# Norm hand-overs, a halved first load, routing by counting, and single waits in a two-block fp32r transformer kernel on one core

## The chip, the cores and the metric
One core of a Trainium2 chip (trn2) runs the whole program in one launch. The metric is the device time in microseconds. Three timed runs of the kernel before gave 1406.56, 1406.8 and 1409.7 us; the median is 1406.8. A separate profiled execution took 1410.64 us, with a span of 1408.7 us from its first to its last instruction.

## The reference, cut to what matters
256 tokens of width 1024 pass through two blocks of two layers each, all in f32.

```python
x = x + even_mix(rms_norm(x, even_norm) @ even_w_in) @ even_w_out        # two attentions, 16 heads each
x = x + odd_mix(rms_norm(x, odd_norm) @ odd_w_in) @ odd_w_out            # retention, 4 heads
x = rms_norm(x, final_norm)
h = layer_norm(x, ln_in_g, ln_in_b)
for l in range(2):
    h = layer_norm(ALPHA * h + hybrid_mixer(h, ...), ln1_g[l], ln1_b[l])
    f = swiglu(h, ffn_wg, ffn_wu, ffn_wd) if l == 0 else moe_swiglu(h, router, wg, wu, wd)
    h = layer_norm(ALPHA * h + f, ln2_g[l], ln2_b[l])

# moe_swiglu: top 2 of 8 experts per token
logits = h @ w_router
top_v, top_i = lax.top_k(logits, 2)
w_top = softmax(top_v)
out = sum over e of gate[:, e] * swiglu(h, wg[e], wu[e], wd[e])
```

## The kernel before
All weights lie in the order of their use as 275 slots of 128 x 2048 f32 (1 MB). A slot is loaded by SP into a raw buffer (two buffers before the experts, four in them). ScalarE (ACT) rounds it to fp32r (`w_hi`), VectorE (DVE) subtracts to get the rest (`w_lo`), and TensorE (PE) multiplies three pairs of parts: hi x hi, lo x hi, hi x lo (`parts_mm`, L592 to L594). Activations are split the same way into `x_hi`, `x_lo` and `y_hi`, `y_lo`. Four decoded slots exist at a time, three in the expert stage. SP may load a raw buffer again once `w_lo` of its last slot is made. Each engine's program is written out by hand in its own order; `ahead(s)` on ACT and on DVE prepares the slot four (three) places later and waits until PE has used the slot that stood there. So the place of an `ahead` call decides which other work of that engine stands behind a late weight.

PE also issues filler matmuls whose results nobody reads: `keep_busy` (L611) around the norms, with counts in `BUSY`, and nine at the start (L891).

Seven norms lie between the stages. Norm 1 (after the even layer) and norm 2 (after the odd layer) are done by `residual_norm`, norms 3 to 5 by `scaled_norm`; both end in `rest_of_norm`. There are two tiles of 128 tokens (t) and two halves of 512 columns (b). For each, DVE adds the matmul result (`joined`), sums (`summed`), and per tile asks POOL for a root (`ready`), centres (`centre`), scales (`finish`, which counts `n_h`); PE turns the rows (`turn_rows_of`), ACT makes `x_hi` (`hi_x`, `n_hi`), DVE makes `x_lo` (`low_part`, `n_lo`), and the next stage's matmuls begin in `begin`. For norm 2 DVE also squares and multiplies by `final_gain` before the statistics.

Other places that the change touches. Start: `const`, `xT`, slot 0, slot 1 and `x` are loaded in this order. After slots 0 to 3, PE needs `small_lo` for 32 narrow matmuls (`small_rows`), then slot 4, then `fold_rows(0)`, which waits for ACT's copy `rows24` (L1385). Even layer output: PE waits for `y_split` of 8 ahead of output slots 4 and 5. Odd layer: ACT copies the value banks at every second V slot (L1418); PE waits for `r_lo` of 4 ahead of the output slots. Sparse layers: DVE makes the low part of the convolution (`conv_low`, L2197). Dense feed-forward: `hidden` (L2240) and `ahead` in turns. Experts: after `fold_rows(3)` the router (`router`) finds the first and the second largest logit with ties by rank, counts tokens per expert through a matmul, and `select` builds the gather matrix; then the first expert slots run. End: `z` and the output of tile 0, then of tile 1 (L2363, L2368).

## Time and profile before

| | |
|---|---|
| median of three timed runs | 1406.8 us |
| profiled execution | 1410.64 us |
| its span | 1408.7 us |
| PE busy | 1366.6 us (97%) |
| DVE, ACT busy | 979.3 us (70%), 764.3 us (54%) |
| HBM read | 304.03 MB |
| filler matmuls at the norms (L611) | 100 |
| mean granted TensorE clock | 0.992 |

A PE matmul of 512 columns shows a duration near 0.39 us, but matmuls overlap. The distance from start to start is what a matmul costs. PEclk 1.00 is 2.4 GHz and 0.50 is 1.2 GHz.

### The profile page before, as it was taken

The page shows a single profiled execution, that of the slowest core. Times are in us where ns is not written, and L with a number is a line of the kernel's source. Part 1 is how long each engine was busy: PE and PEld are TensorE (multiplying, and loading weights), DVE is VectorE, ACT ScalarE, POOL GpSimd, SP SyncE. Part 2 cuts the span into 40 slices and gives each one's busy share as a digit, 9 for nine tenths or more (in the row PEclk, how much of TensorE's full clock was granted, in tenths as well). Part 3 has the DMA queues.
Part 4 walks back from the last instruction along what each step waited for, and adds up shares of the span by engine and source line. Part 5 has one row for each costly group of instructions (what it writes and reads, how often), then busy time and mean ns, then how long its engine had stood idle before and what let it go on. Part 6 is the DMA issues. An engine that isn't in the chain of part 4 may idle for free.

```text
span 1408.7 us, 21698 instructions
## 1 busy us (share of the span) xinstructions
PE 1366.6 (97%) x8601; PEld 1191.2 (85%) x8601; DVE 979.3 (70%) x1369; ACT 764.3 (54%) x925; POOL 95.5 (7%) x114
## 2 busy tenths in 40 slices
PE   7899999999999999999999999999999999999996
PEld 7899888778987889888999889877888888888884
DVE  5546567454767477867544466767988888898887
ACT  4455479335323327743433336753776677677673
POOL 0000023100001110000222010001000000000000
PEclk9899999999999999999999999999999999999998
DMA  7553443435543535534554536442998899989886
GB/s 274 195 180 122 148 150 120 158 145 207 209 149 137 215 147 183 180 116 159 204 184 180 205 122 245 159 142 101 348 334 335 328 335 342 344 324 357 342 327 247
DMA packets 44102, 306.30 MB, mean 217 GB/s; under 512 B 4912, under 2 KB 5168, under 8 KB 8176
## 3 DMA queue, kind: packets, MB, share of 16 engines
q1 hardware_dynamic: 41760, 296.22, 56.9%
q0 software_dynamic: 2256, 8.88, 1.8%
q8 instruction: 60, 0.98, 0.3%
q14 instruction: 26, 0.21, 0.0%
HBM read 304.03 MB, written 1.05 MB: 217 GB/s over the span
## 4 chain that ended last, share of the span: by engine, by line
PE 77%; DVE 10%; DMA 6%; ACT 4%; issue 3%; POOL 1%; SPq 0%; DVEq 0%; ACTq 0%
PE g_ps L592 17%; PE g_ps L594 17%; PE g_ps L593 17%; DMA raw<-w_dram 6%; PE a_ps L597 5%; PE a_ps L592 5%; PE a_ps L594 5%; PE a_ps L593 5%; DVE w_lo L1643 3%; PE a_ps L601 2%; ACT w_hi L1273 2%; PE o_ps L597 2%; DVE x L1777 1%; DVE tiny L1690 1%; POOL tiny L500 1%
## 5 line engine op out<-in xcount | busy, mean ns | idle before, releaser
L1643 DVE TENSOR_TENSOR w_lo<-raw,w_hi 128x2048 fp32r<-128x2048 f32 x239 | 549.0, 2301 | 207.7 <-ACT w_hi L1273 206.0
L1273 ACT ACTIVATE w_hi<-raw 128x2048 fp32r<-128x2048 f32 x239 | 457.5, 1914 | 279.9 <-PE g_ps L594 100.8
L592 PE MATMUL g_ps<-x_hi,w_hi 128*128 128x256 f32 x880 | 253.3, 288 | 0.0
L593 PE MATMUL g_ps<-x_lo,w_hi 128*128 128x256 f32 x880 | 250.4, 285 | 0.0
L594 PE MATMUL g_ps<-x_hi,w_lo 128*128 128x256 f32 x880 | 250.2, 284 | 0.0
L592 PE MATMUL g_ps<-w_hi,x_hi 128*128 128x512 f32 (+1 forms) x552 | 209.2, 379 | 5.5 <-DVE x_lo L1740 3.7
L594 PE MATMUL g_ps<-w_hi,x_lo 128*128 128x512 f32 (+1 forms) x552 | 204.2, 370 | 0.0
L593 PE MATMUL g_ps<-w_lo,x_hi 128*128 128x512 f32 (+1 forms) x552 | 203.9, 369 | 0.0
L592 PEld LDWEIGHTS g_ps<-x_hi,w_hi 128*128 128x128 f32 x880 | 170.4, 194 | 4.1 <-issue 3.9
L593 PEld LDWEIGHTS g_ps<-x_lo,w_hi 128*128 128x128 f32 x880 | 170.4, 194 | 0.0
L594 PEld LDWEIGHTS g_ps<-x_hi,w_lo 128*128 128x128 f32 x880 | 170.3, 194 | 0.0
L592 PE MATMUL a_ps<-w_hi,y_hi 128*128 128x512 f32 x384 | 152.0, 396 | 3.5 <-issue 1.3
L594 PE MATMUL a_ps<-w_hi,y_lo 128*128 128x512 f32 x384 | 149.8, 390 | 0.0
L593 PE MATMUL a_ps<-w_lo,y_hi 128*128 128x512 f32 x384 | 149.7, 390 | 0.0
L592 PEld LDWEIGHTS g_ps<-w_hi,x_hi 128*128 128x128 f32 x552 | 104.4, 189 | 26.0 <-issue 4.5
L594 PEld LDWEIGHTS g_ps<-w_hi,x_lo 128*128 128x128 f32 x552 | 104.4, 189 | 18.3
L593 PEld LDWEIGHTS g_ps<-w_lo,x_hi 128*128 128x128 f32 x552 | 104.5, 189 | 16.4 <-issue 0.2
L1643 DVE TENSOR_TENSOR w_in_raw<-raw,w_in_raw 128x2048 fp32r<-128x2048 f32 x35 | 80.2, 2290 | 52.4 <-ACT w_in_raw L1273 52.3
L592 PEld LDWEIGHTS a_ps<-w_hi,y_hi 128*128 128x128 f32 x384 | 72.1, 188 | 20.0 <-issue 3.8
L1273 ACT ACTIVATE w_in_raw<-raw 128x2048 fp32r<-128x2048 f32 x35 | 66.9, 1910 | 35.3 <-DMA raw<-w_dram 17.0
L594 PEld LDWEIGHTS a_ps<-w_hi,y_lo 128*128 128x128 f32 x384 | 72.1, 188 | 15.5
L593 PEld LDWEIGHTS a_ps<-w_lo,y_hi 128*128 128x128 f32 x384 | 72.2, 188 | 14.2
(323 smaller groups left out, 1985.7 us busy)
## 6 DMA issues: line engine op xcount, KB each, us to landing
raw<-w_dram SPq DMA_DIRECT2D x279, 1024.0 KB, 4.9
arena<-rows_dram POOLq DMA_DIRECT2D x3, 1024.0 KB, 5.3
arena<-xT_dram SPq DMA_DIRECT2D x2, 512.0 KB, 5.1
x<-x_dram SPq DMA_DIRECT2D x2, 512.0 KB, 10.1
extra<-extra_dram POOLq DMA_DIRECT2D x1, 1024.0 KB, 5.1
extra<-rows_dram POOLq DMA_DIRECT2D x2, 512.0 KB, 3.9
y_spare<-rows_dram POOLq DMA_DIRECT2D x4, 256.0 KB, 4.3
...
```

The source lines that it names most:

```text
L500: pool.tensor_tensor(tiny[:, 228 + t0:228 + t0 + n], tiny[:, 224 + t0:224 + t0 + n], tiny[:, 226 + t0:226 + t0 + n], ALU.pow).then_inc(roo ...
L592: pe.matmul(ps, lh, rh, start=start, stop=False, skip_group_check=True)
L593: pe.matmul(ps, lh, rl, start=False, stop=False, skip_group_check=True)
L594: return pe.matmul(ps, ll, rh, start=False, stop=stop, skip_group_check=True)
L597: return pe.matmul(ps, lhs, rhs, start=start, stop=stop, skip_group_check=True)
L601: return pe.transpose(ps, src, ident)
L1273: act.activation(w_hi[w_place(s)][:, :], raw[PLACE[s]][:, :], ACT.Copy).then_inc(hi_done, 1)
L1643: dve.tensor_tensor(w_lo[w_place(s)][:, :], raw[PLACE[s]][:, :], w_hi[w_place(s)][:, :].bitcast(F32), ALU.subtract).then_inc(lo_done, 1)
L1690: own(dve.bn_stats(tiny[:, 200 + 12 * t + 6 * b:206 + 12 * t + 6 * b], xs))
L1777: own(dve.scalar_tensor_tensor(xs, xs, scale, out_bank(t, b)[:, :], ALU.mult, ALU.add))
```

## The change
The kernel after differs in these parts. (1) Slot 0 is loaded in two halves of 512 KB, in turns with the halves of `xT`; ACT and DVE make the parts of input and weight half by half; five fillers instead of nine. (2) ACT prepares slots 4 and 6 later in its order, and copies `rows24` before slot 6; DVE makes `small_lo` before two other waits. (3) PE's waits on `y_split` and `r_lo` are per output slot. (4) Norm 1, norm 2 and norm 3 are written out in new orders; in norm 2 the squares go to ACT; filler counts of norms 2 and 3 fall from 22+11 to 8+4 and from 12 to 5. (5) In the V slots ACT copies before it prepares. (6) `conv_low(0)` moves one step ahead. (7) The first two `hidden` of the dense feed-forward come before the two `ahead`. (8) The router compares all pairs of logits and counts the larger ones; the softmax weights are made in `gate_weights`, behind the two `ahead` calls and in front of the clearing of `f_acc`. (9) At the end both `z` tiles come before the two roots.

```diff
-        BUSY = {2: (22, 11, L_IN[0] + 2), 3: (0, 12, FFN_IN + 2), 4: (0, 12, L_IN[1] + 2), 5: (0, 12, None)}
+        BUSY = {2: (8, 4, L_IN[0] + 2), 3: (0, 5, FFN_IN + 2), 4: (0, 12, L_IN[1] + 2), 5: (0, 12, None)}
...
                 sp.dma_start(xT[:, 4 * b:4 * b + 4, :], a["xT"][:, 4 * b:4 * b + 4, :]).then_inc(xT_in[b], 16)
-            load(0, 0)
+                half = slice(b * SLOT // 2, (b + 1) * SLOT // 2)
+                sp.dma_start(raw[0][:, half], a["w"][0][:, half]).then_inc((half_in, raw_in[0])[b], 16)
...
-            for _ in range(9):
+            for _ in range(5):
...
-            pe.wait_ge(y_split, 8)
+                pe.wait_ge(y_split, 2 * OUT_EVEN[n][0] + 2)
...
-            pe.wait_ge(r_lo, 4)
...
-            act.wait_ge(raw_in[0], 16)
-            act.activation(w_hi[0][:, 0:SLOT // 2], raw[0][:, 0:SLOT // 2], ACT.Copy).then_inc(half_hi, 1)
-            act.activation(w_hi[0][:, SLOT // 2:], raw[0][:, SLOT // 2:], ACT.Copy).then_inc(hi_done, 1)
+            for b in range(2):
+                act.wait_ge(xT_in[b], 16)
+                for k in range(4 * b, 4 * b + 4):
+                    act.activation(y_hi[:, k, :], xT[:, k, :], ACT.Copy, scale=norm_col[:, k:k + 1]).then_inc(u_hi, 1)
+                half = slice(b * SLOT // 2, (b + 1) * SLOT // 2)
+                act.wait_ge((half_in, raw_in[0])[b], 16)
+                act.activation(w_hi[0][:, half], raw[0][:, half], ACT.Copy).then_inc((half_hi, hi_done)[b], 1)
-            even_slot(0)
+            even_slot(0, False)
...
-            for s in range(1, 4):
-                even_slot(s)
+            ahead(0)
+            even_slot(1)
+            even_slot(2, False)
             act.wait_ge(narrow_full, 1)
             act.activation(rows24, a_ps[0][0:48, 0:S], ACT.Copy).then_inc(rows_copied, 1)
-            even_slot(4)
+            ahead(2)
+            for s in range(3, 5):
+                even_slot(s)
...
-                    for n in ((m - 1, m) if m == 1 else (m,)):
+                    for n in (m - 1, m):
-                elif m:
-                    ahead(OD_V + m)
...
+            def squares_of(t, b):
+                act.wait_ge(added, 2 * b + t + 1)
+                act.activation(y_spare[t][:, 16 + 2 * b:18 + 2 * b, :].rearrange("p a b -> p (a b)"),
+                               x[:, t, 512 * b:512 * b + 512], ACT.Square, scale=D ** -0.5,
+                               accum_out=tiny[:, 196 + 2 * t + b:197 + 2 * t + b]).then_inc(squared, 1)
+            for t, b in ((0, 0), (1, 0), (0, 1)):
+                squares_of(t, b)
+            squares_of(1, 1)
...
-                    for m in range(FT):
+                    for m in range(2):
+                        hidden(m)
+                    for m in range(2):
+                        ahead(FFN_IN + m)
+                    for m in range(2, FT):
...
-                    act.wait_ge(m_d, 1)
-                    act.activation(tiny[:, 100:102], tiny[:, 98:100], ACT.Exp).then_inc(m_exp, 1)
...
+                    act.wait_ge(m_d, 1)
+                    act.activation(tiny[:, 100:102], tiny[:, 98:100], ACT.Exp).then_inc(m_exp, 1)
...
+            def plus(t, b):
+                xs = x[:, t, cols(b)]
+                return dve.tensor_tensor(xs, xs, out_bank(t, b)[:, :], ALU.add)
+            def norm_after_even():
+                ahead(EV_OUT + 4)
+                dve.wait_ge(odd_gain_in, 16)
+                dve.wait_ge(used, EV_OUT + 6)
                 for t in range(NT):
+                    joined(1, t, 0, 1.0)
+                ahead(EV_OUT + 5)
+                dve.wait_ge(o_full, O_FULL[1] + 1)
+                joined(1, 0, 1, 1.0)
+                ready(1, 0)
+                finish(1, 0)
+                dve.wait_ge(used, EV_OUT + 8)
+                own(plus(1, 1))
+                low_half(1, 0, 0)
+                own.sync()
+                summed(1, 1, 1)
+                ready(1, 1)
+                low_half(1, 0, 1)
+                finish(1, 1)
+                low_part(1, 1)
+                for n in (6, 7):
+                    ahead(EV_OUT + n)
+            def norm_after_odd(between):
+                def times_gain(t, b):
+                    xs = x[:, t, cols(b)]
+                    dve.wait_ge(squared, 2 * b + t + 1)
+                    own(dve.tensor_tensor(xs, xs, final_gain[:, cols(b)], ALU.mult))
+                    own.sync()
+                for n in range(5):
+                    ahead(OD_OUT + n)
+                    between(n)
+                dve.wait_ge(rows_in, ROWS_IN[2])
+                dve.wait_ge(used, OD_OUT + 6)
+                for t in range(NT):
+                    plus(t, 0).then_inc(added, 1)
+                ahead(OD_OUT + 5)
+                times_gain(0, 0)
+                summed(2, 0, 0)
+                dve.wait_ge(o_full, O_FULL[2] + 1)
+                plus(0, 1).then_inc(added, 1)
+                times_gain(1, 0)
+                times_gain(0, 1)
+                summed(2, 0, 1)
+                ready(2, 0)
+                centre(2, 0)
+                summed(2, 1, 0)
+                finish(2, 0)
+                dve.wait_ge(used, OD_OUT + 8)
+                plus(1, 1).then_inc(added, 1)
+                low_part(2, 0)
+                times_gain(1, 1)
+                summed(2, 1, 1)
+                ready(2, 1)
+                centre(2, 1)
+                finish(2, 1)
+                low_part(2, 1)
+                for n in (6, 7):
+                    ahead(OD_OUT + n)
             def scaled_norm(i, last, full):
                 dve.wait_ge(n_h, 4 * i)
+                def half(t, b):
+                    dve.wait_ge(*full[2 * t + b])
+                    joined(i, t, b, ALPHA)
+                for b in range(2):
+                    half(0, b)
+                ready(i, 0)
+                centre(i, 0)
+                finish(i, 0)
+                half(1, 0)
+                if i == 3:
+                    low_half(i, 0, 0)
+                half(1, 1)
+                if i == 3:
+                    low_half(i, 0, 1)
+                ready(i, 1)
+                if i == 4:
+                    low_part(i, 0)
+                centre(i, 1)
+                finish(i, 1)
+                if i == 5:
+                    low_part(i, 0)
+                low_part(i, 1)
+                for s in () if i == 5 else (last, last + 1):
+                    ahead(s)
...
+                on, on1, on2, lg = t3(16), t3(32), t3(48), t3(112)
+                flat = prob[:, :, :].rearrange("p a b -> p (a b)")
+                above, equal = (flat[:, c:c + NT * NE * NE].rearrange("p (t e o) -> p t e o", t=NT, e=NE) for c in (512, 640))
+                earlier = flat[:, 768:768 + NE * NE].rearrange("p (e o) -> p e o", e=NE)
+                order = const[:, C_RANK:C_RANK + NE]
+                place, pair = t3(80), [P, NT, NE, NE]
+                own(dve.tensor_tensor(earlier, order.unsqueeze(1).to_broadcast([P, NE, NE]),
+                                      order.unsqueeze(2).to_broadcast([P, NE, NE]), ALU.is_gt))
                 dve.wait_ge(m_thi, NT)
                 dve.tensor_tensor(t_lo[:, 1, :], x[:, 1, :], t_hi[:, 1, :].bitcast(F32), ALU.subtract).then_inc(m_tlo, 1)
                 dve.wait_ge(rows_folded, 2 + DEPTH)
                 chain(lambda: dve.tensor_copy(lg, a_ps[1][:, 0:64].rearrange("p (a b) -> p a b", a=2)[:, :, HF:HF + NE]))
+                mine, other = lg.unsqueeze(3).to_broadcast(pair), lg.unsqueeze(2).to_broadcast(pair)
+                own(dve.tensor_tensor(above, other, mine, ALU.is_gt))
+                chain(lambda: dve.tensor_tensor(equal, other, mine, ALU.is_equal),
+                      lambda: dve.tensor_tensor(equal, equal, earlier.unsqueeze(1).to_broadcast(pair), ALU.mult),
+                      lambda: dve.tensor_tensor(above, above, equal, ALU.add),
+                      lambda: dve.tensor_reduce(place, above, AX.X, ALU.add))
+                dve.tensor_scalar(on, place, 2.0, None, ALU.is_lt).then_inc(m_on, 1)
+                own(dve.tensor_scalar(on1, place, 0.0, None, ALU.is_equal))
+                own(dve.tensor_scalar(on2, place, 1.0, None, ALU.is_equal))
+                dve.wait_ge(m_rank, 1)
+                chain(lambda: dve.tensor_tensor(gate, a_ps[1][:, 0:32].rearrange("p (a b) -> p a b", a=2)[:, :, 0:NE], on, ALU.mult),
+                      lambda: dve.tensor_scalar(ranks[:, 0, :, 0:NE], gate, -1.0, None, ALU.add),
+                      lambda: dve.tensor_reduce(most, a_ps[1][0:1, 32:32 + NE], AX.X, ALU.max))
+            def gate_weights():
+                on1, on2, lg = (t3(at) for at in (32, 48, 112))
+                mx = [tiny[:, c:c + 2] for c in (92, 94)]
+                chain(lambda: dve.tensor_reduce(mx[0], lg, AX.X, ALU.max),
+                      lambda: dve.scalar_tensor_tensor(lg, on1, NEG, lg, ALU.mult, ALU.add),
+                      lambda: dve.tensor_reduce(mx[1], lg, AX.X, ALU.max))
                 dve.tensor_tensor(tiny[:, 98:100], mx[1], mx[0], ALU.subtract).then_inc(m_d, 1)
                 dve.wait_ge(m_exp, 1)
                 w1_, w2_, den = tiny[:, 102:104], tiny[:, 104:106], tiny[:, 106:108]
                 chain(lambda: dve.tensor_scalar(den, tiny[:, 100:102], 1.0, None, ALU.add),
...
                       lambda: dve.tensor_tensor(on2, on2, wide(w2_), ALU.mult))
                 for half in range(2):
                     own(dve.tensor_tensor(ranks[:, 1, :, half * NE:(half + 1) * NE], on1, on2, ALU.add))
+                own.sync()
+                dve.tensor_copy(ranks_now[:, 1, :, :], ranks[:, 1, :, 0:2]).then_inc(m_now, 1)
...
-                dve.tensor_copy(ranks_now[:, :, :, :], ranks[:, :, :, at]).then_inc(m_now, 1)
-                dve.wait_ge(m_now, 1 + count)
+                if count is None:
+                    chain(lambda: dve.tensor_copy(ranks_now[:, 0, :, :], ranks[:, 0, :, at]))
+                else:
...
+            for b in range(2):
+                for k in range(4 * b, 4 * b + 4):
+                    dve.wait_ge(u_hi, k + 1)
+                    dve.scalar_tensor_tensor(y_lo[:, k, :], xT[:, k, :], norm_col[:, k:k + 1], y_hi[:, k, :].bitcast(F32),
+                                             ALU.mult, ALU.subtract).then_inc(u_lo, 1)
+                half = slice(b * SLOT // 2, (b + 1) * SLOT // 2)
+                dve.wait_ge((half_hi, hi_done)[b], 1)
+                dve.tensor_tensor(w_lo[0][:, half], raw[0][:, half], w_hi[0][:, half].bitcast(F32),
+                                  ALU.subtract).then_inc((half_lo, lo_done)[b], 1)
...
+            dve.wait_ge(small_hi_done, 1)
+            dve.tensor_tensor(small_lo, small_raw, small_hi.bitcast(F32), ALU.subtract).then_inc(small_done, 1)
-            dve.wait_ge(small_hi_done, 1)
-            dve.tensor_tensor(small_lo, small_raw, small_hi.bitcast(F32), ALU.subtract).then_inc(small_done, 1)
...
-                            conv_low(0)
+                        if m == I_B[0]:
+                            conv_low(0)
...
-                    for m in range(FT):
+                    for m in range(2):
+                        hidden(m)
+                    for m in range(2):
+                        ahead(FFN_IN + m)
+                    for m in range(2, FT):
...
                     next_x(q, q + 1, a_ps[q])
                 ahead(L_WO[1] + 3)
                 chain(lambda: dve.tensor_scalar(ranks[:, 0, :, NE:2 * NE], gate, -1.0 - P, None, ALU.add))
+                gate_weights()
                 dve.memset(f_acc[:, :, :], 0.0).then_inc(m_acc, 1)
...
+                own.sync()
+                for t in range(NT):
+                    own(dve.scalar_tensor_tensor(z[:, t, :], x[:, t, :], end_mean[:, t:t + 1], gain_of(6), ALU.add, ALU.mult))
+                own.sync()
-                    own.sync()
-                    own(dve.scalar_tensor_tensor(z[:, t, :], x[:, t, :], end_mean[:, t:t + 1], gain_of(6), ALU.add, ALU.mult))
...
```

## Rows read from the trace of the kernel before

**Rows 1.** The page: busy time of each engine, and the DMA share by slices.
```profile
PE 1366.6 (97%) x8601; PEld 1191.2 (85%) x8601; DVE 979.3 (70%) x1369; ACT 764.3 (54%) x925; POOL 95.5 (7%) x114
...
DMA  7553443435543535534554536442998899989886
```
**Rows 2.** Waits of PE: who released it, us in total, times, longest.
```profile
PE g_ps L592 <- DVE x_lo L1740: 4.1, 6, 1.6
PE a_ps L597 <- ACT prob L1385: 2.8, 1, 2.8
PE a_ps L592 <- DVE y_lo L2197: 2.6, 4, 1.0
PE a_ps L740 <- DVE small L1996: 2.0, 1, 2.0
...
PE a_ps L592 <- issue: 1.3, 1, 1.3
...
PE o_ps L601 <- DVE part L2240: 1.1, 1, 1.1
PE a_ps L592 <- DVE y_lo L2051: 0.9, 1, 0.9
PE g_ps L592 <- ACT arena L1418: 0.9, 1, 0.9
```
**Rows 3.** Windows: stretch, length, busy by engine, granted clock, DMA share, GB/s.
```profile
9.00:10.00 1.00, 1.00 (x3) 0.72 (x3) 0.84 (x3) 0.60 (x2) 0.00 (x0) 1.00 1.01 426
38.00:42.50 4.50, 4.50 (x41) 4.50 (x39) 3.80 (x2) 0.53 (x2) 0.00 (x0) 0.62 0.66 227
49.80:56.00 6.20, 6.20 (x28) 6.15 (x29) 2.49 (x2) 2.32 (x2) 0.00 (x0) 0.50 0.82 324
58.00:62.00 4.00, 4.00 (x35) 4.00 (x35) 0.92 (x5) 3.33 (x5) 0.00 (x0) 1.00 0.73 252
301.00:305.50 4.50, 4.50 (x14) 3.51 (x14) 2.03 (x6) 0.60 (x1) 0.60 (x1) 0.62 0.17 35
```
**Rows 4.** Timeline of ACT, first 50 us: start, length, what, idle before and releaser.
```profile
9.66 1.06 ACT L1367 ACTIVATE w_hi<-raw 128x1024 fp32r<-128x1024 f32 x1 [0.40 <-DMA raw<-w_dram]
...
30.89 1.91 ACT L1273 ACTIVATE w_hi<-raw 128x2048 fp32r<-128x2048 f32 x1 [6.86 <-DMA raw<-w_dram]
...
49.37 0.36 ACT L1385 ACTIVATE prob<-a_ps 48x256 f32<-48x256 f32 x1
```
**Rows 5.** Timeline of PE: the first weight matmul.
```profile
12.03 0.38 PE L592 MATMUL g_ps<-w_hi,y_hi 128*128 128x256 f32 x1 [0.21 <-DVE w_lo L1969]
```
**Rows 6.** Timeline of DVE, first 50 us: parts of slots 2, 4 and 5.
```profile
20.78 2.29 DVE L1643 TENSOR_TENSOR w_lo<-raw,w_hi 128x2048 fp32r<-128x2048 f32 x1
...
37.31 4.49 DVE L1643 TENSOR_TENSOR w_lo<-raw,w_hi 128x2048 fp32r<-128x2048 f32 x2
```
**Rows 7.** Line L611, the fillers: count, duration in ns, first and last start.
```profile
L611 PE MATMUL g_ps<-small x100: 387/389/500, 502.5 to 983.0; 128*128 128x512 f32 x100
```
**Rows 8.** Group of DVE instructions: count, busy us, mean ns of one.
```profile
L1777 DVE SCALAR_TENSOR_TENSOR x<-x,a_ps 128x512 f32<-128x512 f32 x20 | 13.5, 677 | 0.0
```
**Rows 9.** Timeline of norm 2: DVE's scaling of tile 0.
```profile
507.24 1.42 DVE L1730 SCALAR_TENSOR_TENSOR x<-x,tiny,arena 128x512 f32<-128x512 f32 x2
```
**Rows 10.** Timeline of norm 2: PE's first weight matmul.
```profile
512.70 0.36 PE L592 MATMUL g_ps<-w_hi,x_hi 128*128 128x256 f32 x1 [0.78 <-DVE x_lo L1740]
```
**Rows 11.** Timeline of ACT at the end: a square of 1024 columns.
```profile
1397.98 1.15 ACT L1629 ACTIVATE y_spare<-x,tiny 128x1024 f32<-128x1024 f32 x1 [3.14 <-DVE tiny L2343]
```
**Rows 12.** Timeline of DVE after the router: clearing `f_acc`, then the fourth expert slot.
```profile
991.49 1.76 DVE L2272 MEMSET arena<- 128x2048 f32 x1 [0.49 <-DVE extra L2271]
993.17 2.23 DVE L1643 TENSOR_TENSOR w_lo<-raw,w_hi 128x2048 fp32r<-128x2048 f32 x1
```
**Rows 13.** Timeline of ACT after the router: the fourth expert slot.
```profile
990.25 1.92 ACT L1273 ACTIVATE w_hi<-raw 128x2048 fp32r<-128x2048 f32 x1 [2.26 <-PE g_ps L594]
```
**Rows 14.** Timeline of DVE at the end: last of three refining steps.
```profile
1404.57 0.16 DVE L1664 SCALAR_TENSOR_TENSOR tiny<-tiny 128x1 f32<-128x1 f32 x1
```

109 lines of the change are left out of this document (24 added, 85 removed).

## The prediction
> **What bounds the kernel now.** I read the page first: PE is busy 1366.6 of 1408.7 us [rows 1], so TensorE's own order is the path nearly everywhere, and no change of DVE or ACT counts unless PE waits for it. Second, PE's waits, to see where it stands still and for whom [rows 2]. Third, the windows around these places, to see the granted clock: three stretches right behind idle time ran at 0.62, 0.50 and 0.62 of full speed on average [rows 3]. Fourth, the timelines of single engines, to see what a late instruction stood behind [rows 4 to 6, 9 to 14]. The reader is to see two sorts of hidden cost: an idle PE is paid once as a gap, and again when the clock granted behind it is the lower level (1.2 GHz). A third sort counts as busy: 100 filler matmuls [rows 7]. Start to start, 35 matmuls of 256 columns took 4.00 us at clock 1.00, 28 took 6.20 us at 0.50 [rows 3]; I take 0.12 us and 0.23 us for one, and 5.8 us for a slot of 48 such matmuls. A 512-column matmul costs twice that: 0.23 us, 5.4 us for an output slot of 24.
>
> **The change part by part**, in PE's time.
>
> Start. The first matmul begins at 12.03 when the low part of half a slot is ready [rows 5]; ACT began that half at 9.66 on the landing of the whole 1 MB [rows 4]. With halves in turns, the first weight half lands behind one half of xT. ACT does four input pieces, then the weight half from about 7.6, and DVE's part is done near 9.9: PE starts some 2 us earlier. But slot 2's low part still starts at 20.78 and lasts 2.29 [rows 6], because it stands behind the norm statistics of x, which nothing here moves. Before, slot 2 began on PE at 12.03 + 2 x 5.8 + 0.2 = 23.8; now it can begin at 23.1. Gain 0.7, between 0 and 2. Cutting the fillers to five costs nothing in the sum: I take full pace to come near 12 us as before, so some real matmuls run slowly, inside the time that slot 2 waits for anyway.
> The Trainium skill (TensorE: Matmul & The Clock Gate, "What's actually happening") says the warm-up is a budget of time and not a number of matmuls. The fillers ran slowly here (3 in 1.00 us [rows 3], where 4 to 5 fit at full pace); by the rule the four dropped ones are paid by slot 0 at the same pace, about 0.9 us, which is less than the 2 us gained and changes nothing behind slot 2.
> DMA share was 1.01 at 426 GB/s while 512 KB and 1 MB transfers stood in the queue together [rows 3], so I let the halves stream without a gap. The skill (DMA: Bandwidth & Descriptors, "Measured (HBM→SBUF...)") advises transfers of 1 MiB or more, and its Anatomy section gives about 2.0 us fixed cost for each; were this paid in series, slot 1 would land 2 us late. That is a rival below.
>
> Slots 3 to 7, the largest term. ACT's preparation of slot 4 sat in the queue until its load landed at 30.89 [rows 4], and the rounding of x stood behind it; so the narrow matmuls waited 2.0 for small_lo [rows 2] and low parts 4 and 5 began at 37.31 [rows 6]. Now x_hi, small_hi and x_lo are done near 31, ahead of the end of slot 3 (34.6). Gain: gap 2.0, and the half clock of 38 to 42.5 [rows 3], (1 - 0.62) x 4.5 = 1.7; less the start's 0.7 nothing, since both move together. Low part 4 comes at 35 instead of 39.6, slot 6's load, which waits for it, comes 4.5 us sooner, and the copy rows24 no longer stands behind slot 6's rounding. Before, the copy came at 49.37 [rows 4] and PE had waited 2.8 [rows 2]; now it comes at 37, during slot 4. Gain 2.8 and the half clock of 49.8 to 56 [rows 3], 0.50 x 6.2 = 3.1, together 2.0 + 1.7 + 2.8 + 3.1 = 9.6. No late weight takes its place: I followed loads, rounding and low parts of slots 5 to 9, and each is ready 3 us or more before its slot. Bounds: 5 (one of the stalls stays) and 10.5.
>
> Even layer's end. Output slot 4 needs y_split of 6 only, so the wait for DVE's last part, 0.9 [rows 2] and 0.2 of pipeline refill, goes: 1.1. In norm 1 tile 0's first half is joined one output slot earlier, and the second tile's sum is moved behind the first x_lo; z is ready when PE ends, and its first next matmul comes 2.0 instead of 2.9 us behind: 0.9. The longest wait for x_lo, 1.6 [rows 2], falls to about 0.8, a length behind which no slow stretch is found elsewhere (0.9, 1.1 and 1.3 in rows 2), so 0.38 x 4.5 = 1.7 [rows 3] goes too. Together 3.7; bounds 1.5 and 4.5.
>
> Value slots. ACT copied behind a rounding that waited for a load; PE waited 0.9 [rows 2]. Gain 0.9 (0 to 1.4). The prepared slots come later, but a V slot lasts 5.4 us and copy, two roundings and a low part 1.1 + 3.8 + 2.3 = 7.2 us, with 10.8 to spare.
>
> Odd output. r_lo of 2 is enough for the first slot: the 1.3 "issue" wait [rows 2] goes. Gain 1.3 (1.0 to 1.5).
>
> Norm 2. PE's last output matmul ends at T = 502.5, where the fillers start [rows 7]; DVE's scaling starts at T + 4.7 [rows 9], since four pieces of add, square, gain and statistics (0.68 to 0.70 each [rows 8]) ran in a row; the next weight matmul starts at T + 10.2 [rows 10]. In the new order the pieces of half 0 are added a slot earlier, squares are on ACT, and only add, gain and statistics of (0,1) follow the third output slot. A square of 512 columns isn't in the trace: 1.15 for 1024 columns [rows 11] bounds it from above, 0.5 from below, and I take 0.7 with its sum; it costs DVE 0.1 of waiting, at most 0.6. I get scaling at T + 1.2, x_lo at T + 4.0, so the first weight matmul comes 6.2 earlier, for which 12 fillers instead of 33 just leave room. But tile 1 is late: gain, statistics, root, centring, refining and scaling follow the x_lo of tile 0, so its rows are ready at T + 9.2 and PE waits 1.8. The second tile's matmuls start at T + 10.6; before it was T + 15.6 (10.2, 2.9 for 24 matmuls, 1.9 for narrow ones and turns, 0.6 of waiting): gain 5.0; bounds 2 and 6.5.
>
> Norm 3 and feed-forward. The first x_lo moves ahead of the last join: first matmul 1.9 earlier, second tile 1.2 earlier, which stays. The first two hidden before the weights remove PE's wait of 1.1 [rows 2]. Gain 2.3 (1 to 3). Norms 4 and 5 keep their order: 0.
>
> conv_low: the first part comes sooner, but the second half of the slot waits for the second y_lo, whose chain is as long as before. Of the 2.6 in [rows 2] nothing is won: 0 (-3.4 for two clock drops, +1).
>
> Router. Six operations on 128 elements take the place of ten on 16; each costs 0.17 to 0.68 [rows 8]. Whichever, PE has 12 fillers to run (2.7 us) and m_on just reaches their end; the weights' softmax leaves the path to select. Gain 0.4. It comes back in a worse place: gate_weights (12 small operations and a round trip to ACT, 2.6 us) stands before the clearing of f_acc at 991.49, behind which the low part of expert slot 3 ran at 993.17 to 995.40 [rows 12], just when PE came to it (no wait for it stands in rows 2). ACT's rounding at 990.25 [rows 13] now waits for the exp too. I get 997.4, with PE there 0.4 sooner than before: a new wait of 2.4, net -2.0 (-0.5 to -3).
>
> End. Moving the second z before the refining removes one such wait: three steps of 0.16 to 0.2 [rows 14], 0.6 (0 to 0.7).
>
> Sum: 0.7 + 9.6 + 3.7 + 0.9 + 1.3 + 5.0 + 2.3 + 0.4 - 2.4 + 0.6 = 22.1. Two new waits, 1.8 in norm 2 and 2.4 in the experts, are longer than the 1.6 behind which the clock fell; I charge 1.7 each: 18.7. The profiled execution of 1410.6 would become 1391.9; against the median 1406.8, 3.8 lower, I predict 1388.1.
>
> **The rivals.**
> (a) The clock does not fall behind the new waits. For it: 1.3 passed unpunished. Against: 1.6, 2.0 and 2.8 did not. Time 1384.7.
> (b) Half of the first stage's gain stays away, because the two stalls change into waits for loads (ACT's idle before slot 4 is 6.86, a DMA [rows 4]). Against: that load is not what PE waited for. 1388.1 + 4.8 = 1393.
> (c) The halved load pays a fixed cost in series; slot 1 and all loads behind it come 2 us late: 1390.
> (d) Slower. The experts turn from PE-bound to weight-bound: the DMA share is 0.9 to 1.0 in all their slices [rows 1], and gate_weights takes the ring's reserve at their start. If the low parts then stayed behind PE, each of 132 slots would pay; from 0.15 us a slot on it eats the 18.7, and at 0.2 the time is 1388 + 26 = 1414. Against: among PE's waits no w_lo row is long enough to stand in [rows 2], so the ring has slack and refills.
> (e) The waits on norm 2 don't shorten because DVE stands waiting for ACT's squares, whose order puts slot 5's rounding first: gain 2 instead of 5, 1391.
>
> **How the numbers follow.** Forecast 0.45, (a) 0.2, (b) 0.15, (c) 0.04, (e) 0.1, (d) 0.03, something unseen of either sign 0.03. A difference of 0.3% (4.2 us) is about what a measurement of this kernel tells from none. All cases but (d) and half of the unseen are faster by more: 0.95; same 0.02, slower 0.03. Range 1381 to 1396: below (a) by two of the unsure gains, above (b) by 3.
>
> **What would show it.** Right: first weight matmul near 10.0 and slot 2 near 23.1; no PE wait for small or rows24, clock 1.00 up to 300 us; PE at the first V slot 14 us earlier; from fillers to the first weight matmul of norm 2 about 4 us; a new PE wait near 2.4 us for w_lo within 12 us of the expert slots' start. Wrong: a PE wait for w_lo in slots 4 to 9, waits for w_lo spread over the experts, or an expert stage longer by more than 5 us.

## The result, and the profile after

| | before | after |
|---|---|---|
| median of four timed runs | 1408.0 us (1406.6 to 1409.7) | 1392.35 us (1391.0 to 1393.1) |
| profiled execution, span | 1410.6, 1408.7 us | 1392.1, 1390.3 us |
| mean granted TensorE clock, that execution | 0.992 | 0.996 |
| PE busy | 1366.6 us | 1354.7 us |
| filler matmuls at the norms | 100 | 72 |

The ratio is 0.9887 (95% interval 0.9870 to 0.9904): faster by 1.0 to 1.3%. The forecast was 1388.1 with a range of 1381 to 1396.

First the waits of PE in the trace of after, to be held against [rows 2]:

```profile
PE g_ps L594 <- DVE w_lo L1663: 4.0, 5, 2.3
PE a_ps L594 <- DVE y_lo L2283: 2.6, 2, 1.3
PE g_ps L594 <- DVE x_lo L1755: 2.6, 5, 1.1
PE a_ps L603 <- DVE x L1746: 2.6, 2, 1.8
```

`small` and `prob` are gone, and so are the 1.3 of "issue", the 0.9 of `y_split`, the 0.9 of the value copies and the 1.1 of `part`. `x_lo` fell from 4.1 to 2.6, `y_lo` of the convolution stayed at 2.6 (two waits of 1.3 where four made it up). Two waits are new: 1.8 for `x`, tile 1 of norm 2 (with 0.8 of an old one, 2.6 in all), and 2.3 for `w_lo`, expert slot 3. Expert slots are counted from 0, so slot 3 is the fourth, that of [rows 12].

Then the windows, first those of [rows 3] and two stretches behind the new waits (columns as there):

```profile
38.00:42.50 4.50, 4.50 (x40) 4.50 (x39) 0.31 (x1) 1.88 (x3) 0.00 (x0) 1.00 0.90 353
49.80:56.00 6.20, 6.20 (x54) 6.20 (x53) 3.19 (x7) 2.92 (x3) 0.00 (x0) 1.00 0.49 156
288.00:296.00 8.00, 6.93 (x37) 5.62 (x36) 5.13 (x12) 3.48 (x4) 1.16 (x2) 1.00 0.18 40
495.00:500.00 5.00, 3.16 (x29) 2.92 (x30) 3.96 (x8) 2.65 (x3) 2.93 (x5) 1.00 0.00 0
975.50:979.00 3.50, 3.50 (x10) 2.72 (x9) 3.50 (x2) 0.93 (x1) 0.00 (x0) 0.51 0.80 264
```

The granted clock is the third figure from the end: 1.00 in the first stage and behind norm 1, also behind the 1.8 us wait of norm 2, and 0.51 behind the wait of the experts.

The sum by stages is read from PE's own instructions: each matmul of before is paired with the same one of after, and the difference of their starts is written down at a few marks. What changes between two marks was won or lost there.

| stretch of before (us) | ahead at its end | won in it, measured | predicted |
|---|---|---|---|
| start, to slot 2 (30) | -0.2 | -0.2 | 0.7 |
| slots 3 to 7 (60) | 9.1 | 9.3 | 9.6 |
| end of even layer, norm 1 (320) | 12.7 | 3.6 | 3.7 |
| value slots (345) | 14.3 | 1.6 | 0.9 |
| odd output, `r_lo` (495) | 15.4 | 1.1 | 1.3 |
| norm 2 (520) | 19.7 | 4.3 | 5.0, less 1.7 for the clock |
| norm 3, feed-forward, layer 2 (900) | 22.1 | 2.3 | 2.3 |
| norm 5, router (992) | 22.75 | 0.7 | 0.4 |
| expert slot 3 (1010) | 18.7 | -4.1 | -2.4, less 1.7 for the clock |
| rest of the experts (1390) | 18.15 | -0.5 | 0 |
| end (span) | 18.4 | 0.25 | 0.6 |

The profiled execution became 18.5 us shorter; 18.7 were forecast.

The lines that answer to [rows 4 to 6] show why the start won nothing. ACT's rounding of slots 1 and 2, then DVE's low part of slot 2, then PE's first weight matmul and its first of slot 2 (the prediction had 10.0 and 23.1):

```profile
12.85 1.92 ACT L1276 ACTIVATE w_hi<-raw 128x2048 fp32r<-128x2048 f32 x1 [1.08 <-DMA raw<-w_dram]
19.64 1.92 ACT L1276 ACTIVATE w_hi<-raw 128x2048 fp32r<-128x2048 f32 x1 [4.87 <-DMA raw<-w_dram]
```
```profile
21.58 2.29 DVE L1663 TENSOR_TENSOR w_lo<-raw,w_hi 128x2048 fp32r<-128x2048 f32 x1
```
```profile
9.27 0.49 PE L594 MATMUL g_ps<-w_hi,y_hi 128*128 128x256 f32 x1
...
23.93 0.39 PE L594 MATMUL g_ps<-w_hi,y_hi 128*128 128x256 f32 x1 [0.55 <-DVE w_lo L1663]
```

Slot 0 began 2.8 earlier (12.03 in [rows 5]), but slot 2's low part begins 0.8 later than in [rows 6], where it stood behind the norm statistics; now it stands behind ACT's rounding of the same slot (19.64 + 1.92 = 21.56), which waited for its load.

Norm 2 answers to [rows 9, 10]. PE's last output matmul ended at T = 487.1. DVE, with the length of each step, and PE's first weight matmul of either tile:

```profile
487.69 1.41 DVE L1746 SCALAR_TENSOR_TENSOR x<-x,tiny,arena 128x512 f32<-128x512 f32 x2
489.02 0.68 DVE L1786 TENSOR_TENSOR x<-x,a_ps 128x512 f32<-128x512 f32 x1
490.17 1.29 DVE L1755 TENSOR_TENSOR x_lo<-a_ps,x_hi 128x512 fp32r<-128x512 f32 x2 [0.47 <-ACT x_hi L1294]
491.38 0.68 DVE L1817 TENSOR_TENSOR x<-x,arena 128x512 f32<-128x512 f32 x1
...
493.22 1.27 DVE L1733 SCALAR_TENSOR_TENSOR x<-x,tiny,arena 128x1024 f32<-128x1024 f32 x1
494.96 0.16 DVE L1682 SCALAR_TENSOR_TENSOR tiny<-tiny 128x1 f32<-128x1 f32 x1 [0.46 <-POOL tiny L502]
...
495.54 1.42 DVE L1746 SCALAR_TENSOR_TENSOR x<-x,tiny,arena 128x512 f32<-128x512 f32 x2
```
```profile
491.01 0.36 PE L594 MATMUL g_ps<-w_hi,x_hi 128*128 128x256 f32 x1
...
498.42 0.39 PE L594 MATMUL g_ps<-w_hi,x_hi 128*128 128x256 f32 x1 [0.50 <-DVE x_lo L1755]
```

Tile 0's scaling came at T + 0.6 (before T + 4.7), the first weight matmul at T + 3.9 (10.2), the second tile's at T + 11.3 (15.6).

Behind the router, to [rows 12, 13], DVE on its way to the low part of expert slot 3:

```profile
968.31 0.17 DVE L1921 TENSOR_REDUCE tiny<-tiny 128x2 f32<-128x16 f32 x1
...
970.67 0.17 DVE L1935 COPY extra<-extra 128x4 f32<-128x4 f32 x1
971.21 1.76 DVE L2363 MEMSET arena<- 128x2048 f32 x1 [0.37 <-issue]
972.89 2.23 DVE L1663 TENSOR_TENSOR w_lo<-raw,w_hi 128x2048 fp32r<-128x2048 f32 x1
```

The gate weights stand from 968.31 to 970.84, then the clearing, then the low part, 20.28 ahead of before (993.17) where PE is 22.75 ahead. The difference is PE's wait of 2.3, within 0.2.

### The profile page after: what moved, and what is told of

Its sections match the earlier page's. It is cut to its first block, busy times and chain, and to the rows that moved or that the text cites. A ratio compares the mean times of both kernels' runs of the same rounds, so it can differ in the third digit from the quotient of the medians.

```text
span 1390.3 us, 21637 instructions
## 1 busy us (share of the span) xinstructions
PE 1354.7 (97%) x8569; PEld 1182.7 (85%) x8569; DVE 977.7 (70%) x1362; ACT 767.2 (55%) x933; POOL 98.5 (7%) x114
## 3 DMA queue, kind: packets, MB, share of 16 engines
HBM read 304.03 MB, written 1.05 MB: 219 GB/s over the span
## 4 chain that ended last, share of the span: by engine, by line
PE 81%; DVE 9%; DMA 4%; ACT 3%; issue 2%; POOL 1%; SPq 0%; DVEq 0%; ACTq 0%
PE g_ps L594 18%; PE g_ps L596 18%; PE g_ps L595 18%; PE a_ps L594 5%; PE a_ps L596 5%; PE a_ps L595 5%; PE a_ps L599 5%; DMA raw<-w_dram 4%; DVE w_lo L1663 3%; PE a_ps L603 2%; PE o_ps L599 2%; ACT w_hi L1276 2%; POOL tiny L502 1%; DVE tiny L1706 1%; PE g_ps L613 1%
## 5 line engine op out<-in xcount | busy, mean ns | idle before, releaser
L596 PEld LDWEIGHTS a_ps<-w_hi,y_lo 128*128 128x128 f32 x384 | 72.1, 188 | 15.5
L595 PEld LDWEIGHTS a_ps<-w_lo,y_hi 128*128 128x128 f32 x384 | 72.2, 188 | 14.3
## 6 DMA issues: line engine op xcount, KB each, us to landing
x<-x_dram SPq DMA_DIRECT2D x2, 512.0 KB, 10.6
```

Source lines behind the costliest of these rows:

```text
L595: pe.matmul(ps, lh, rl, start=False, stop=False, skip_group_check=True)
L596: return pe.matmul(ps, ll, rh, start=False, stop=stop, skip_group_check=True)
```

## The experiments

Each runs on the same chip as a fresh series of the kernel before; ratios are to that series. "Ahead" is PE's lead over the trace of before at a mark, read as in the table above. The series ran on several chips, and that of before had medians from 1408.0 to 1409.8 on them; so two kernels from different series are best compared by their ratios, and by medians only within a series.

**The slot order alone.** Onto the kernel before:

```diff
-            even_slot(0)
+            even_slot(0, False)
...
-            for s in range(1, 4):
-                even_slot(s)
+            ahead(0)
+            even_slot(1)
+            even_slot(2, False)
             act.wait_ge(narrow_full, 1)
             act.activation(rows24, a_ps[0][0:48, 0:S], ACT.Copy).then_inc(rows_copied, 1)
-            even_slot(4)
+            ahead(2)
+            for s in range(3, 5):
+                even_slot(s)
...
+            dve.wait_ge(small_hi_done, 1)
+            dve.tensor_tensor(small_lo, small_raw, small_hi.bitcast(F32), ALU.subtract).then_inc(small_done, 1)
             dve.wait_ge(vec_in, 16)
             dve.wait_ge(const_in, 16)
...
-            dve.wait_ge(small_hi_done, 1)
-            dve.tensor_tensor(small_lo, small_raw, small_hi.bitcast(F32), ALU.subtract).then_inc(small_done, 1)
```


> The kernel before with one part of the change alone: ACT rounds x and the narrow weights ahead of slot 4's rounding, copies the narrow rows ahead of slot 6's, and DVE makes the low narrow part before the fold constants. Theory (the prediction's step): the waits of 2.00 and 2.85 us and both stretches at half clock go, without any help of the halved first load. After against before gained 9.0 us between PE's slot 2 and slot 6, so I expect 9 here too: no PE wait over 0.5 between 24 and 60 us, clock 1.00 there, and about 1408.0 - 9 = 1399. Rival: the order needs the earlier start, and a wait for a load or low part of 2 us or more takes the place of one of the two; then 1403 or more.

Measured 1400.66, ratio 0.9941 (0.9926 to 0.9956). PE lost 0.5 to the start and then won 9.3 between 30 and 60 us, the same 9.3 as in the changed kernel. Its windows, the first two those of the stalls, the third behind norm 1:

```profile
38.00:42.50 4.50, 4.50 (x39) 4.50 (x39) 1.35 (x2) 2.52 (x3) 0.00 (x0) 1.00 0.84 317
49.80:56.00 6.20, 6.20 (x54) 6.20 (x54) 3.19 (x7) 3.00 (x3) 0.00 (x0) 1.00 0.57 209
292.00:296.50 4.50, 4.50 (x21) 3.70 (x22) 2.25 (x6) 0.81 (x1) 0.60 (x1) 1.00 0.13 22
```

The rival is out: the order needs no earlier start. The 8.0 us of the medians (an interval of 6.2 to 10.4) is less than the 9 expected and agrees with it. The third line was not expected. Norm 1 is that of before here, PE waited the same 1.6 us for `x_lo`, and the clock stayed at 1.00 where [rows 3] has 0.62.

**The two waits kept, but filled.** Onto the kernel before, on PE:

```diff
             for s in range(2, 4):
                 plain_slot(s)
+            for _ in range(8):
+                pe.matmul(a_ps[2][:, :], early[:, 0:P], early[:, :], start=True, stop=True, skip_group_check=True)
             pe.wait_ge(n_lo, 4)
...
             even_slot(4)
+            for _ in range(12):
+                pe.matmul(a_ps[2][:, :], early[:, 0:P], early[:, :], start=True, stop=True, skip_group_check=True)
             fold_rows(0)
```


> The kernel before with the two waits of the first stage kept, but filled: 8 filler matmuls of 512 columns (1.8 us) ahead of the narrow matmuls, 12 (2.7 us) ahead of the fold. Theory A (the prediction's step): each wait of 2.0 and 2.85 is followed by half clock in every execution; then the fillers give back 1.7 + 3.1 = 4.8 us, clock 1.00 from 24 to 60 us, and the time is 1408.7 - 4.8 = 1403.9. Theory B: the half clock comes behind such a wait in some executions only (after norm 1 the same wait of 1.61 us was followed by it in the trace of before and not in that of the slot order alone); then the typical gain is 0 to 3 us, 1406 to 1408.5, though this trace still shows clock 1.00 there.

Measured 1404.39 against 1409.77, ratio 0.9962 (0.9950 to 0.9973): 5.4 us (3.8 to 7.0), with 4.2 won between 30 and 60 us of its trace. The granted clock shows 1.00 in both places, and its mean was 0.996 to 0.997 in all eight runs against 0.993 to 0.995 in the twelve of before. So nearly half of the largest term, 4.2 of 9.3 in the traces, was the clock, by a test in which no weight came sooner. Whether it falls behind both waits in every execution (theory A) is less sure. The times agree with 4.8, but the mean clocks differ by 0.0023 on average, which over 1408 us is about 3.2 (an estimate), and in another series four of the eleven runs of before had 0.996. So it fell often behind these waits, and not surely each time.

**The old start.** In the changed kernel, both halves of xT, then slot 0 in one load; nine fillers.

```diff
-                half = slice(b * SLOT // 2, (b + 1) * SLOT // 2)
-                sp.dma_start(raw[0][:, half], a["w"][0][:, half]).then_inc((half_in, raw_in[0])[b], 16)
+            load(0, 0)
```


> The changed kernel with the old start: both halves of xT, then slot 0 in one load, the rounding in the old order, nine fillers. The predicted gain of 0.7 at slot 2 did not come: PE began slot 2 at 23.93, before at 23.77. Theory A: the halved load is paid later (slot 1's rounding began at 12.85 against 12.14, slot 2's at 19.64 against 18.23), so with the old start slot 2 begins at about 23.8, slots 1 and 2 are rounded at about 12.1 and 18.2, and the time is within 0.5 us of the changed kernel, 1392.3. Theory B (the halves are worth what was predicted, and something else in the changed order ate it): slot 2 begins at 24.6 and the time is 1393.0 or more.

**Slot 0 whole, between the halves.**

```diff
-                half = slice(b * SLOT // 2, (b + 1) * SLOT // 2)
-                sp.dma_start(raw[0][:, half], a["w"][0][:, half]).then_inc((half_in, raw_in[0])[b], 16)
+                if b == 0:
+                    load(0, 0)
```


> The changed kernel with slot 0 loaded as one transfer of 1 MB between the two halves of xT. Theory A1: what delays slots 1 and 2 is the halved load (the windows 6 to 8 us show 238 and 291 GB/s at a DMA share of 1.0, before 418 and 426); then slot 1's rounding begins near 12.1, slot 2's near 18.2, the first weight matmul near 10.5, slot 2 on PE near 23.1 behind its low part, and the time is about 1391.5. Theory A2: it is the order (weights ahead of the second half of xT), not the size; then slots 1 and 2 come as late as in the changed kernel (12.85 and 19.64), slot 2 on PE at 23.9, 1392.3 again.

Measured 1393.09 (0.9865 to 0.9900) and 1392.74 (0.9872 to 0.9906): neither differs from the changed kernel. ACT's rounding of slots 1 and 2 with the old start:

```profile
12.06 1.91 ACT L1275 ACTIVATE w_hi<-raw 128x2048 fp32r<-128x2048 f32 x1 [0.48 <-DMA raw<-w_dram]
18.18 1.91 ACT L1275 ACTIVATE w_hi<-raw 128x2048 fp32r<-128x2048 f32 x1 [4.21 <-DMA raw<-w_dram]
```

Theory A holds for the loads: in the four traces with the old start slot 2's rounding began at 18.05 to 18.23, in the seven with halves at 19.46 to 20.42. It fails for what they are worth. With the old start PE began slot 2 at 23.6 to 25.4 (the expectation had 23.8, and the run itself gave 25.4) although the low part was ready at 22.9 to 23.1, because PE itself was late: matmuls of 256 columns came every 0.21 us first and every 0.12 later, and the moment of the change lay anywhere from 11.8 (or a little sooner, in a pause) to 16.1 us in the 13 traces, with the first filler at 6.9 to 8.1. With halves, PE waited up to 1.0 for the low part instead. PE's lead over the trace of before at 30 us: old start 0.0 (before itself), -0.5, -1.6, +0.2; halves -0.2, -0.4, -0.5, 0.0, -0.1, -0.4, -0.95; whole slot between -0.3, -1.4. All three are worth the same within what the start varies by. Of A1 and A2, the rate of the loads speaks for A1. From 6 to 8 us, in the changed kernel and in the run with the whole slot between:

```profile
6.00:8.00 2.00, 1.03 (x3) 0.84 (x4) 1.61 (x5) 1.86 (x4) 0.00 (x0) 1.00 0.98 264
```
```profile
6.00:8.00 2.00, 0.59 (x1) 0.50 (x2) 1.67 (x4) 1.36 (x4) 0.00 (x0) 1.00 0.99 408
```

The last figure is GB/s: 254 to 279 in all seven traces with halves, 393 to 422 in all six with slot 0 in one load, in whichever place. What is left open is slot 2's rounding: with the whole slot between it came at 18.65 in one trace and at 19.41 in the other, later than with the old start in both.

**The old norm 2.** The changed kernel with the old chain, written out:

```diff
                 for t in range(NT):
-                    plus(t, 0).then_inc(added, 1)
-                ahead(OD_OUT + 5)
-                times_gain(0, 0)
-                summed(2, 0, 0)
+                    joined(2, t, 0, 1.0)
                 dve.wait_ge(o_full, O_FULL[2] + 1)
...
+                joined(2, 0, 1, 1.0)
...
-        BUSY = {2: (8, 4, L_IN[0] + 2), 3: (0, 5, FFN_IN + 2), 4: (0, 12, L_IN[1] + 2), 5: (0, 12, None)}
+        BUSY = {2: (22, 11, L_IN[0] + 2), 3: (0, 5, FFN_IN + 2), 4: (0, 12, L_IN[1] + 2), 5: (0, 12, None)}
```


> The changed kernel with the old order of norm 2 alone: squares on DVE, each piece joined, squared, gained and measured in one go, fillers 22 and 11. The step was sized 5.0 at the second tile's matmuls; PE's marks in the two traces give 19.72 - 15.43 = 4.3. Theory: it stands alone, so PE loses 4.3 at 520 us against the changed kernel and all of it to the end, 1396.7. Rival: part of the gain was made possible by the r_lo and even-layer edits ahead of it or is taken back behind it; then the loss at the end is under 3.

Measured 1396.75, ratio 0.9906 (0.9891 to 0.9921). At 495 us PE was 15.6 ahead and at 520 us 15.6: nothing was won, where the changed kernel wins 4.3. Up to the experts nothing of it is taken back: from 520 to 992 us PE won 3.3 here and 3.0 in the changed kernel. Whether all of it reaches the end is not shown. The trace lost another 3.8 behind 1010 us, and by the ratios (0.9906 against 0.9887 and 0.9884) the loss is 2.7 to 3.1 us, with an interval of 2 us to either side of each ratio, by medians of different series 3.5 to 4.4; the rival's "under 3" is not out.

**The old end of the even layer.**

```diff
+            pe.wait_ge(y_split, 8)
             for n in range(4, 6):
-                pe.wait_ge(y_split, 2 * OUT_EVEN[n][0] + 2)
...
                 dve.wait_ge(used, EV_OUT + 8)
-                own(plus(1, 1))
-                low_half(1, 0, 0)
-                own.sync()
-                summed(1, 1, 1)
+                joined(1, 1, 1, 1.0)
                 ready(1, 1)
-                low_half(1, 0, 1)
+                low_part(1, 0)
```


> The changed kernel with the old end of the even layer: one wait for all eight parts ahead of output slot 4, and norm 1 in its old order. Sized 1.1 + 0.9 in waits and 1.7 in clock. Theory A: the waits return (0.94 for y_split and 1.61 for x_lo), and 1.2 + 0.8 = 2.0 us are lost at 320 us, with or without a stretch at half clock behind the second; time 1394.4, or 1396 if the clock falls each time. Rival B: norm 1's new order brings nothing by itself, since both waits end on DVE's chain; then 1.2 is lost.

Measured 1396.04, ratio 0.9908 (0.9893 to 0.9923). The waits of 0.95 and 1.61 are back, and between the marks at 60 and 320 us PE won 1.6, where the traces of the changed order won 3.6: 2.0 us, the 1.2 and 0.8 of theory A. Rival B, 1.2, is out, and norm 1's wait shows where the 0.8 lies: 1.61 here, 1.07 in the changed order. Behind the 1.61 the clock stayed at 1.00 in this trace too. The 1.6 that is won here all the same was also won by the slot order alone and by the filled run, with norm 1 untouched: it is what the trace of before lost to half clock behind this wait, in that one execution. The medians differ by more, 2.8 to 3.7, within what these series scatter (its four runs lie between 1391.3 and 1397.4).

**The gate weights later.** In the changed kernel, the whole of them and ACT's exp moved into the experts. The expectation names the slots at whose turn the pieces stand; the low part made just ahead of each is three slots further, that of expert slot 6, 8 and 10:

```diff
-                gate_weights()
-                dve.memset(f_acc[:, :, :], 0.0).then_inc(m_acc, 1)
...
                         ahead(s + 1, i)
+                        if not earlier and u == 1:
+                            gate_weights()
+                        if not earlier and u == 2:
+                            gate_weights_from_exp()
+                        if not earlier and u == 3:
+                            dve.memset(f_acc[:, :, :], 0.0).then_inc(m_acc, 1)
```


> The changed kernel with the softmax of the two gate weights taken out of DVE's way into the experts: its first part behind expert slot 3's low part, the second behind slot 5's, the clearing of the sum behind slot 7's, and ACT's exp with them. Theory: PE's wait of 2.33 us for the low part of expert slot 3 goes, and with it the stretch of 3.4 us at half clock behind it (1.7 us): 4.0 us, about 1388.3, and no PE wait over 0.5 in the first ten expert slots. Rival: DVE has no slack there, and the work moved down delays slots 5 to 8 instead; then PE waits 1 to 2.5 us one or two slots later and the gain is under 1.5 us.

Measured 1393.53, ratio 0.9890 (0.9875 to 0.9906): no gain. The wait of 2.3 went, and PE waited 1.12, 0.53 and 1.05 at 988, 992 and 999 us. The rival got the result, and ACT's timeline shows a reason that neither had:

```profile
981.00 1.28 ACT L1603 ACT_TABLE_LOAD   x1
982.30 0.20 ACT L1603 ACTIVATE tiny<-tiny 128x2 f32<-128x2 f32 x1
...
982.79 1.28 ACT L1612 ACT_TABLE_LOAD   x1
984.09 0.38 ACT L1612 ACTIVATE prob<-g_ps 128x256 f32<-128x256 f32 x1
```

An exp between two Silus brought two loads of tables, 2.6 us that the roundings behind it came late. PE's first wait, 1.12, ends on the low part of slot 8 (986.31), which had waited 1.39 for such a rounding. The other two stand right behind what was moved on DVE, the second part of the gate weights (988.52 to 989.99) and the clearing (995.43, 1.76 us); so this run alone does not tell the rival's reason from this one.

**The gate weights split.** The operations up to the difference go where DVE waits for the ranks, so the exp runs ahead of the first Silu as before; the other eight go behind the low part of expert slot 10 (at the turn of slot 7; the expectation says 11); GpSimd clears the sum.

```diff
                 own(dve.tensor_scalar(on2, place, 1.0, None, ALU.is_equal))
+                own.sync()
+                gate_difference()
                 dve.wait_ge(m_rank, 1)
...
                         ahead(s + 1, i)
+                        if not earlier and u == 3:
+                            gate_weights()
...
                     load_both_rows(6)
+                    pool.wait_ge(m_on, 1)
+                    pool.memset(f_acc[:, :, :], 0.0).then_inc(m_acc, 1)
```


> The changed kernel with the gate weights split: their four operations up to the difference stand where DVE waits for the ranks (idle 1.65 us there), so ACT's exp comes before the experts' activations as in the kernel before, the other eight stand behind the low part of expert slot 11, and the sum is cleared by GpSimd. Theory: in the run with the gate weights later, ACT loaded its tables twice more, 1.28 us each at 981.00 and 982.79, and that gave the three new waits of PE (1.12, 0.53, 1.05); without it no PE wait over 0.5 stands in the first twelve expert slots, PE is some 3 to 4 us ahead of the changed kernel at 1030 us, 1388.5. Rival: DVE is so nearly full there (4.5 of 5 us) that eight operations (1.6 us) anywhere in the first slots come back as a wait; gain under 2 us.

Measured 1388.83, ratio 0.9855 (0.9840 to 0.9870). DVE's last of the four operations, the first behind the wait for the ranks, and the low part of expert slot 3, which began 3.2 earlier than in the changed kernel:

```profile
958.06 0.16 DVE L1927 TENSOR_TENSOR tiny<-tiny 128x2 f32<-128x2 f32 x1
959.05 0.17 DVE L1916 TENSOR_TENSOR tiny<-a_ps,tiny 128x16 f32<-128x16 f32 x1 [0.83 <-PE a_ps L601]
...
969.73 2.29 DVE L1664 TENSOR_TENSOR w_lo<-raw,w_hi 128x2048 fp32r<-128x2048 f32 x1 [1.24 <-issue]
```

PE's longest wait from 955 to 1350 us was 0.50, and it was 22.7 ahead at 1010 and 1030 us, where the changed kernel is 18.7, or 20.2 in the trace of it in which the clock did not fall there. The rival is out: the eight operations came back as no wait. The run moves three things at once, so it does not share out the gain among them.

**The changed kernel again, only the clearing moved, and both improvements.** Three kernels on one chip:

> The changed kernel once more, as the measure for the two beside it on the same chip. Expected 1392.4 within 1; in its trace the wait of 1.76 us in norm 2 without a stretch at half clock behind it, as in all traces so far that have it, and the wait of 2.3 us in the experts with or without one (3 of 5 traces so far had it).

> The changed kernel with only the clearing of the experts' sum moved from DVE to GpSimd; the gate weights stay where the change put them. Theory: PE's wait for the low part of expert slot 3 is the sum of what stands ahead of it on DVE, gate weights 2.6 us and clearing 1.76; the clearing alone cost no wait in the kernel before. Without it the low part begins at about 971.2 instead of 972.89 and PE's wait falls from 2.33 to about 0.6, with no half clock behind; time 1392.4 - 1.7 - 1.0 (the clock in 3 of 5) = 1389.7. Rival: the wait is set by ACT's rounding behind the exp (it began at 969.24 and lasts 1.9); then the low part can't begin before 971.2 either and the figure is the same, but taking the gate weights away gains no more than this. The split run shows 967.73 for that rounding.

> The changed kernel with the gate weights split and the sum cleared by GpSimd, and slot 0 loaded whole between the halves of xT. Against the changed kernel beside it: 3.6 us from the experts (2.3 of wait, 1.7 of clock in 3 of 5 traces, 0.2 from the router); from the start nothing that can be told, since slot 2 began on PE 0 to 1.6 us late against the trace of before with the same old start, and 0 to 0.5 late with either new one. 1388.8.

Measured 1393.21 (1390.7 to 1395.9), 1391.67 (1390.1 to 1393.3) and 1389.79 (1388.7 to 1391.7); ratios 0.9884, 0.9872 and 0.9866, each within 0.0017. With only the clearing moved, the same low part and PE's wait for it:

```profile
971.91 2.29 DVE L1665 TENSOR_TENSOR w_lo<-raw,w_hi 128x2048 fp32r<-128x2048 f32 x1 [0.33 <-ACT w_hi L1278]
```
```profile
PE g_ps L596 <- DVE w_lo L1665: 0.9, 2, 0.6
```

The wait fell from 2.3 to 0.65, as the sum says, and the last thing awaited was ACT's rounding, which stood behind the exp: both explanations meet there. The median moved by 1.5 only, less than the 2.7 expected and no more than these series scatter. The eight runs of the two kernels with the gate weights split lie between 1387.6 and 1391.7, mean 1389.4, and the nine of the changed kernel between 1390.7 and 1395.9, mean 1392.6: 3.1 us better than the changed kernel (3.4 by the medians within the last series) and 19 to 21 better than before. The split is the version to keep; the whole slot between the halves adds nothing that can be told.

## Why the prediction was right, and where it was not

The order of the terms held. Slots 3 to 7 carry half of the gain (9.3 for 9.6), and the reason is shown twice: the order alone brings it, and filling the waits brings the clock's part of it (4.2 for 4.8). Norm 3 with the feed-forward, `r_lo`, the convolution's 0, and the wait that the gate weights and the clearing make at expert slot 3 (2.33 for 2.4, and at the predicted slot) came as worked out. Of the rivals, (b), (e) and (d) as stated did not come: no wait for a load replaced the two stalls, ACT's squares cost DVE 0.3 at most, and the experts stayed with PE. Rival (a) came at norm 2 always and at the experts in half of the traces, but without its time of 1384.7.

Four steps failed.

*"longer than the 1.6 behind which the clock fell; I charge 1.7 each."* The prediction took the length of a wait as what decides whether the clock falls behind it, and charged 1.7 for each of the two new ones. The traces together:

| wait | length (us) | half clock behind it |
|---|---|---|
| `small`, rows24 (before) | 2.0, 2.85 | 1 of 1 trace each; often, by the mean clocks beside the filled run |
| `x_lo`, norm 1, old order | 1.61 | 1 of 4 |
| `x`, tile 1 of norm 2 | 1.76 | 0 of 9 |
| `w_lo`, expert slot 3 | 2.3 | 3 of 6 |

So length alone does not decide it: 1.76 was never followed by half clock and 1.61 once. What does is not shown. The charge at norm 2 was wrong in every trace (rival (a) there), that at the experts right in half of them (1.6 where it came), and the gain of 1.7 behind norm 1 belonged to one execution.

That the profiled executions came out at 18.5 for 18.7 is in part luck. At norm 2, 1.7 was charged for nothing, and the value slots and the router gave 1.0 more than sized; against that the start gave 0.9 less, slots 3 to 7 and the odd output 0.5, the second tile of norm 2 0.7, the rest of the experts 0.5 and the end 0.35.

The forecast of 1388.1 missed by 4.3. Of this, 1.2 is the median that it was set off against: 1406.8 from three runs, where before gave 1408.0 to 1409.8 in four series. The other 3.1 is the gain, 18.7 for 15.6 between the medians (1408.0 and 1392.35; 15.5 in the last series). The sum took its clock losses from one execution of before with a mean clock of 0.992, as low as any of the 32 later runs (0.992 to 0.996, median 0.994), and 0.002 of 1408 us is 2.8 (an estimate). The profiled execution of after, with 0.996 where its other three runs had 0.997, gives 1.4 of that back. The remaining 1.7 is within the scatter of the runs and is not explained further.

*"I let the halves stream without a gap"*, and slot 2 "stands behind the norm statistics of x". The halves did not keep the rate: 264 GB/s from 6 to 8 us where before had 422. The roundings of slots 1 and 2 came 0.9 and 1.7 us later on average, in the direction of rival (c), and its consequence was not that of the rival: it only took the place of the statistics as what slot 2 waits for. The 0.7 were not won, nothing that can be told was lost, and the predicted 23.1 was 23.9, although the first matmul came sooner than predicted (9.27 for 10.0).

*"The second tile's matmuls start at T + 10.6."* Tile 1's rows were ready at T + 9.3, as predicted (9.2), with a wait of 1.76 (1.8). From there to the weight matmul it took 2.07 (turning, rounding, low part), and the sum had allowed 1.4: 0.7 too much gain.

*The end*, "three steps of 0.16 to 0.2". The steps went, and something else came. GpSimd's root for tile 0, before and after:

```profile
1400.49 0.57 POOL L585 TENSOR_TENSOR tiny<-tiny 128x1 f32<-128x1 f32 x1
```
```profile
1382.34 1.50 POOL L587 TENSOR_TENSOR tiny<-tiny 128x1 f32<-128x1 f32 x1
```
```profile
1380.92 2.48 DVE L2453 SCALAR_TENSOR_TENSOR arena<-x,tiny,arena 128x1024 f32<-128x1024 f32 x2
```

The third line is DVE in the changed kernel: its second pass of 1.2 us, moved ahead, now runs while GpSimd computes the root, and the root took 1.50 instead of 0.57. The first output came 5.8 us behind PE's end where it had come 4.8; the second 7.7 instead of 7.9. Of 0.6 there remained 0.25. The run with the old norm 2 tests this on another root without having been made for it. In the changed kernel the second root of norm 2 runs beside `centre`, a pass over 1024 columns; with the old norm 2 it runs beside `x_lo`, and its time changes:

```profile
493.38 1.54 POOL L502 TENSOR_TENSOR tiny<-tiny 128x1 f32<-128x1 f32 x1 [6.34 <-DVE tiny L1721]
```
```profile
496.45 0.57 POOL L502 TENSOR_TENSOR tiny<-tiny 128x1 f32<-128x1 f32 x1 [5.41 <-DVE tiny L1716]
```

In the 13 traces all 94 roots beside such a `scalar_tensor_tensor` pass over 1024 columns took 1.50 to 1.55, and all 33 beside an `x_lo` pass 0.55 to 0.57. So the change itself, by moving a pass beside the root, took back most of what it won at the end.

The value slots gave 1.6 for 0.9: 1.2 where the wait of 0.9 stood, with the pipeline's refill, and 0.4 around 340 us, where before had a second, shorter pause that the prediction had not listed.

One reading of the prediction was wrong: that no wait for `w_lo` in the trace of before is long enough to stand beside those of [rows 2]. Two are, both in the experts (at 1381 and 1095 us):

```profile
PE a_ps L592 <- DVE w_lo L1643: 1.2, 1, 1.2
...
PE g_ps L592 <- DVE w_lo L1643: 0.8, 1, 0.8
```

So the experts had less slack than it took them to have. There PE lost 0.5 behind 1010 us in the changed kernel and between -0.9 and 3.8 in the other traces (the run with the gate weights later included), in waits of up to 1.6 for `w_lo`, `x_lo`, `sel` and `part`. So this stretch, with a DMA share of 0.85 to 0.89 on average in five traces, gives back a part of what is won ahead of it, a different part in each execution. It looks like a small form of rival (d), and it can account for most of the scatter of the runs; no run tests either.
